# In the mixer: one channel group's filter moved to ScalarE and GpSimd, the channel norm ahead of the attention units, output halves one per unit

## The reference, cut to what matters

```python
h = xn @ w_in
glu_a, glu_g, c_q, c_kv, k_r = jnp.split(h, SPLIT_EVEN, axis=-1)
u = glu_a * jax.nn.sigmoid(glu_g)
u = causal_dwconv(u, conv_w, conv_b)                    # 31 taps, each channel by itself
u = jax.nn.silu(layer_norm(u, conv_ln_g, conv_ln_b))
q = (rms_norm_2(c_q, q_norm) @ w_uq).reshape(b, s, N_HEADS, 96)
q_nope, q_rope = q[..., :QK_NOPE_DIM], rope(q[..., QK_NOPE_DIM:], pos)
kv = (rms_norm_2(c_kv, kv_norm) @ w_ukv).reshape(b, s, N_HEADS, 128)
k_nope, v = kv[..., :QK_NOPE_DIM], kv[..., QK_NOPE_DIM:]
k_rope = rope(k_r[:, :, None, :], pos)[:, :, 0, :]
attn = mla_attention(q_nope, q_rope, k_nope, k_rope, v)  # causal, 4 blocks of 128 rows
return jnp.concatenate([u, attn], axis=-1) @ w_out
```

## Time and profile before

| | us |
|---|---|
| median of 3 runs | 2725.79 (2721.75 to 2727.71) |
| the profiled execution, its own time | 2724.76 |
| its span, first to last instruction | 2722.3 |
| PE busy in the span | 2653.7 (97%) |
| DVE, ACT, POOL busy | 1329.2, 623.9, 317.1 |
| the mixer's part in question, from 1523.4 to 1731.6 | 208.2 |

### The profile page before, as it was taken

One profiled execution on the slowest core, in us unless ns is written; L12 is line 12 of the kernel. 1 busy time (PEld: TensorE's weight loads), 2 busy tenths in 40 slices (PEclk: granted clock), 3 DMA queues, 4 the chain that ended last, 5 costly groups with the idle time before them and its releaser, 6 DMA issues.

```text
span 2722.3 us, 31881 instructions
## 1 busy us (share of the span) xinstructions
PE 2653.7 (97%) x12378; PEld 1844.2 (68%) x12378; DVE 1329.2 (49%) x2850; ACT 623.9 (23%) x1152; POOL 317.1 (12%) x313
## 2 busy tenths in 40 slices
PE   8999999999999999999999998999999999999998
PEld 4777658898895655444444445588884484888887
DVE  2255556566552013000013776477666673877733
ACT  1155532313321112110001134222220022222201
POOL 0222124434342410000000000000000000000000
PEclk9999989999999998999999998999999999999999
DMA  4211111111012220344433210122223211222222
GB/s 190 78 47 63 47 47 47 43 36 47 32 47 93 94 95 32 124 170 170 170 116 108 78 62 16 70 78 93 93 81 120 96 63 62 78 93 93 78 93 93
DMA packets 32494, 226.98 MB, mean 83 GB/s; under 512 B 3552, under 2 KB 4192, under 8 KB 6112
## 3 DMA queue, kind: packets, MB, share of 16 engines
q1 hardware_dynamic: 30384, 219.50, 22.5%
q10 hardware_dynamic: 1968, 5.51, 0.6%
HBM read 222.90 MB, written 2.10 MB: 83 GB/s over the span
## 4 chain that ended last, share of the span: by engine, by line
PE 92%; DVE 4%; ACT 2%; issue 1%; POOL 0%; DMA 0%; ACTq 0%; DVEq 0%; POOLq 0%
PE psum L400 90%; DVE work L2721 1%; PE psum L899 1%; PE psum L1226 0%; DVE work L1802 0%; PE psum L2248 0%; PE psum L2577 0%; DVE work L1050 0%; DVE hT L572 0%; DVE work L1796 0%; ACT work L613 0%; DMA mixT<-x_dram 0%; PE psum L636 0%; PE psum L1892 0%; ACT work L965 0%
## 5 line engine op out<-in xcount | busy, mean ns | idle before, releaser
L400 PE MATMUL psum<-hT,ring 128*128 128x256 f32 (+2 forms) x2872 | 542.8, 370 | 10.8 <-ACT work L1351 6.1
L400 PEld LDWEIGHTS psum<-hT,ring 128*128 128x128 f32 (+1 forms) x2872 | 375.9, 162 | 143.7 <-issue 95.4
L400 PE MATMUL psum<-work,ring 128*128 128x512 f32 (+1 forms) x1208 | 418.5, 498 | 4.8 <-ACT work L3506 2.4
L400 PEld LDWEIGHTS psum<-work,ring 128*128 128x128 f32 x1208 | 228.3, 190 | 178.7 <-issue 156.4
L400 PE MATMUL psum<-work 128*128 128x128 f32 (+7 forms) x2390 | 326.8, 290 | 10.3 <-ACT work L2682 6.6
L400 PEld LDWEIGHTS psum<-work 128*128 128x128 f32 (+2 forms) x2390 | 275.2, 178 | 62.3 <-issue 31.9
L400 PE MATMUL psum<-work,mixT 128*128 128x256 f32 (+2 forms) x1332 | 289.2, 379 | 2.7 <-ACT work L2101 1.5
L400 PE MATMUL psum<-xT,ring 128*128 128x256 f32 (+1 forms) x1120 | 285.1, 400 | 1.4 <-ACT mixT L754 1.3
L400 PEld LDWEIGHTS psum<-work,mixT 128*128 128x128 f32 (+1 forms) x1332 | 232.1, 182 | 49.2 <-issue 16.1
L400 PE MATMUL psum<-ring,work 128*128 (+1 forms) x568 | 248.7, 596 | 2.2 <-issue 1.9
L400 PEld LDWEIGHTS psum<-xT,ring 128*128 128x128 f32 x1120 | 206.1, 190 | 53.2 <-issue 26.4
(11 more groups left out here) (450 smaller groups left out, 2740.9 us busy)
## 6 DMA issues: line engine op xcount, KB each, us to landing
ring<-stream_dram SPq DMA_DIRECT2D x204, 1024.0 KB, 4.8
con<-consts_dram SPq DMA_DIRECT2D x1, 2953.0 KB, 13.4
mixT<-x_dram ACTq DMA_DIRECT2D x4, 512.0 KB, 6.2
work<-x_dram ACTq DMA_DIRECT2D x4, 512.0 KB, 5.9
out_dram<-mixT SPq DMA_DIRECT2D x4, 512.0 KB, 3.7
work<-p_dram ACTq DMA_DIRECT2D x1, 512.0 KB, 3.9
con<-ssm_dram ACTq DMA_DIRECT2D x1, 512.0 KB, 4.2
vec<-vecs_dram SPq DMA_DIRECT2D x1, 378.0 KB, 5.7
```

Of the source, the lines that this page charges most:

```text
L400: ins = self.eng.matmul(out, lhsT, rhs, start=start, stop=stop)
```

## The change

It touches the mixer alone. Group 1's 31 taps (`POOL_TAPPED = 1`) leave DVE. ACT makes the scaled, shifted copy of each tap (`tap_products`), into one of four buffers, and POOL adds it to `ys` (`taps_pool`), 30 additions in a chain. ACT's 31 products stand behind its gate tiles 1, 2 and 3 and its two query latents, and from tap 5 on each waits until POOL has done tap t-4. The gate and up tiles of group 3 now come right behind those of group 2, and the weight stream has its slots in that order. PE does the diagonal products, the mean, and the sum of squares between the projections instead of in the loop, and the first four output products ahead of unit 0; in the loop it does one output product per unit, to unit 27. DVE subtracts the mean and scales between the rotary additions, and does no tap in the loop. POOL spreads the rotary key over the heads (a copy of 32x4096) in ACT's place.

```diff
-    for j in range(3):
+    for j in range(4):
...
-    gated(3)
...
+        POOL_TAPPED, TAPPED_ORDER = 1, (0, 2, 3)
+        HALF_FIRST, HALF_LAST, TURN_AT = 4, 27, (12, 20, 28)
+        filter_bank = psum[:, 2, :]
...
-            for j in range(1, 3):
-                w = slot()
...
+            for j in range(1, 4):
                 w = slot()
                 tile_pe(blocks(w, 0, 8), h)
                 tile_pe(blocks(w, 8, 8), h)
             w = slot()
             tile_pe(blocks(w, 0, 8), h)
-            for k in range(3):
+            tile_pe(blocks(w, 8, 8), h)
+            e.eng.wait_ge(S["keys_act"], KEYS_STEP["diagonals"])
+            e.eng.wait_ge(S["tile_free"], e.c["tile"].at(-2))
+            for t in range(PE_TAPS):
+                ins = e.mm(filter_bank, diag[:, t, :], upad[:, 3, t:t + T], t == 0, t == PE_TAPS - 1)
+            ins.then_inc(S["ln_pe"], 1)
+            for k in range(2):
                 e.eng.wait_ge(S["squares"], TILES + k + 1)
-                ins = col_sums_pe(e, squares[:, 4 + k, :], mean_col(256 if k < 2 else 128), 0 if k < 2 else NB, k == 0, k == 2)
+                ins = col_sums_pe(e, squares[:, 4 + k, :], mean_col(256), 0, k == 0, k == 1)
             ins.then_inc(S["col_sums"], 1)
+            w = slot()
             e.eng.wait_ge(S["tile_free"], e.c["tile"].at(-1))
             o = e.bank()
...
-                if k == 4:
+                if k == 5:
                     e.eng.wait_ge(S["col_root"], e.c["col_root"].next())
...
-                    root_rows_pe(e, root_bank, 0)
-                    root_rows_pe(e, root_bank2, NB).then_inc(S["mla_root"], 1)
-                ins = e.mm(o, blk(w, 8 + k), h[k], k == 0, k == DC - 1)
+                    root_rows_pe(e, root_bank, 0).then_inc(S["mla_root"], 1)
+                ins = e.mm(o, blk(w, k), h[k], k == 0, k == DC - 1)
             ins.then_inc(S["tile_done"], 1)
+            tile_pe(blocks(w, 8, 8), h)
+            e.eng.wait_ge(S["squares"], TILES + 3)
+            col_sums_pe(e, squares[:, 6, :], mean_col(128), NB, True, True).then_inc(S["col_sums"], 1)
+            for n, j in enumerate((*TAPPED_ORDER[:2], POOL_TAPPED, TAPPED_ORDER[2])):
+                if j == POOL_TAPPED:
+                    e.eng.wait_ge(S["mix_pool"], MIX_POOL["channel"])
+                else:
+                    e.eng.wait_ge(S["channel"], TAPPED_ORDER.index(j) + 1)
+                ins = e.mm(aux_banks[0], mean_of(512), ys[:, j, :], n == 0, n == 3)
+            ins.then_inc(S["ln_pe"], 1)
...
             for n in range(8):
                 tile_pe(blocks(w, 2 * n, 2), [cq[:, k, :] for k in range(2)])
+                if n == 3:
+                    e.eng.wait_ge(S["col_root"], e.c["col_root"].next())
+                    root_rows_pe(e, root_bank2, NB).then_inc(S["mla_root"], 1)
+                if n == 4:
+                    for k in range(4):
+                        e.eng.wait_ge(S["ln_act"], LN_ACT["squares"] + k + 1)
+                        ins = e.mm(aux_banks[0], mean_of(512), squares[:, k, :], k == 0, k == 3)
+                    ins.then_inc(S["ln_pe"], 1)
...
-            e.eng.wait_ge(S["keys_act"], KEYS_STEP["k_spread"])
+            e.eng.wait_ge(S["mix_pool"], MIX_POOL["k_spread"])
             scores(0)
             scores(1)
-            for k in range(3):
-                e.eng.wait_ge(S["channel"], k + 1)
-                e.mm(aux_banks[0], mean_of(512), ys[:, k, :], k == 0, False)
+            e.eng.wait_ge(S["ln_act"], LN_ACT["out"])
+            aux.half_out(e, HALF_FIRST)
...
-                if u < PE_TAPS:
-                    if u == 0:
...
-                    if u == OUT_AT:
-                        e.eng.wait_ge(S["ln_act"], 1 + 4 + 1 + 4)
-                    if u in (22, 26):
-                        aux.turned(e, 1 if u == 22 else 2)
-                    aux.half_out(e, 2)
...
+                if u <= HALF_LAST:
+                    aux.half_out(e, 1)
...
-            for j in range(1, 3):
+            def tap_products(e, first, end):
+                e.eng.wait_ge(S["tile_free"], upad_at)
+                for t in range(first, end):
+                    w = taps_w[:, POOL_TAPPED, t:t + 1]
+                    if t >= 5:
+                        e.eng.wait_ge(S["mix_pool"], MIX_POOL["taps"] + t - 4)
+                    if t == 0:
+                        ins = nc.scalar.activation(ys[:, POOL_TAPPED, :], upad[:, POOL_TAPPED, 0:T], ACT.Identity, scale=w,
+                                                   bias=V("conv0_b")[:, POOL_TAPPED:POOL_TAPPED + 1])
+                    else:
...
+                    ins.then_inc(S["ln_act"], 1)
...
+            for j in range(1, 4):
                 gate(j)
+                if j == POOL_TAPPED:
+                    upad_at = e.c["tile"].at()
+                if j >= POOL_TAPPED:
+                    tap_products(e, *((0, 5), (5, 15), (15, 24))[j - POOL_TAPPED])
             for k, dst in enumerate((cq[:, 0, :], cq[:, 1, :], ckv)):
                 whole(dst)
                 e.eng.wait_ge(S["tile_free"], e.c["tile"].at())
                 nc.scalar.activation(squares[:, 4 + k, :], dst, ACT.Square).then_inc(S["squares"], 1)
+                if k < 2:
+                    tap_products(e, *((24, 29), (29, 31))[k])
+                if k == 1:
+                    col_sqrt_act(e, 0, NB, C("eps")[:, 0:1])
             e.skip(1)
...
+            for k in range(4):
+                e.eng.wait_ge(S["ln_dve"], k + 1)
+                nc.scalar.activation(squares[:, k, :], ys[:, k, :], ACT.Square).then_inc(S["ln_act"], 1)
...
+            for k in range(4):
+                e.eng.wait_ge(S["ln_dve"], LN_DVE["scaled"] + k + 1)
+                nc.scalar.activation(catT[:, k, :], ys[:, k, :], ACT.Silu, bias=V("ln_b")[:, k:k + 1])\
+                    .then_inc(S["ln_act"], 1)
             mla_act(e)
...
+        def taps_pool(e):
+
+            y = ys[:, POOL_TAPPED, :]
+            for t in range(1, 31):
+                e.eng.wait_ge(S["ln_act"], t + 1)
+                if t > 1:
+                    e.eng.wait_ge(S["mix_pool"], MIX_POOL["taps"] + t - 1)
+                nc.gpsimd.tensor_tensor(y, y, squares[:, t % 4, :], ALU.add).then_inc(S["mix_pool"], 1)
+            e.eng.wait_ge(S["rope"], KEY_ROPE)
+            e.eng.wait_ge(S["mix_pool"], MIX_POOL["channel"])
+            nc.gpsimd.tensor_copy(kh[64:96, :, :], bc1(kr[64:96, :], MH)).then_inc(S["mix_pool"], 1)
...
-            e.eng.wait_ge(S["gate_rooted"], 2)
+            e.eng.wait_ge(S["mix_pool"], MIX_POOL["gate_up"])
             gated(0)
+            taps.some(e, 16)
+            gated(1)
+            taps.some(e, 15)
+            gated(2)
             taps.some(e, 17)
-            gated(1)
-            taps.some(e, 17)
-            gated(2)
-            taps.some(e, 34)
+            gated(3)
+            taps.some(e, 14 + 13)
+            col_root_dve(e, 0, NB)
+            taps.some(e, 3)
+            e.eng.wait_ge(S["mla_root"], e.c["mla_root"].next())
+            for k in range(2):
+                nc.vector.scalar_tensor_tensor(out=cq[:, k, :], in0=cq[:, k, :], scalar=V("mla_q")[:, k:k + 1], in1=root_bank,
+                                               op0=ALU.mult, op1=ALU.mult).then_inc(S["latents"], 1)
+            taps.some(e, 7 + 1)
...
-            taps.some(e, 4)
-            e.eng.wait_ge(S["mla_root"], e.c["mla_root"].next())
...
+            e.eng.wait_ge(S["ln_pe"], LN_PE["mean"])
+            for j in range(4):
+                if j == POOL_TAPPED:
+                    e.eng.wait_ge(S["mix_pool"], MIX_POOL["channel"])
+                nc.vector.tensor_tensor(ys[:, j, :], ys[:, j, :], aux_banks[0], ALU.subtract).then_inc(S["ln_dve"], 1)
...
+                if n == 0:
+                    e.eng.wait_ge(S["mla_root"], e.c["mla_root"].next())
+                    nc.vector.scalar_tensor_tensor(out=ckv, in0=ckv, scalar=V("mla_kv"), in1=root_bank2, op0=ALU.mult,
+                                                   op1=ALU.mult).then_inc(S["latents"], 1)
+            e.eng.wait_ge(S["ln_act"], LN_ACT["root"])
+            for j in range(4):
+                nc.vector.scalar_tensor_tensor(out=ys[:, j, :], in0=ys[:, j, :], scalar=V("ln_g")[:, j:j + 1],
+                                               in1=rstd, op0=ALU.mult, op1=ALU.mult).then_inc(S["ln_dve"], 1)
```

More of the change, by code:

```diff
@@ L2452, in program @@
         SO_FAR, TURNED = UNITS_A, UNITS_A + 2 * NB
-        TAPS_AT, MEAN_AT, SUMS_AT, ROOT_AT, OUT_AT = 9, 9, 11, 13, 16
+        LN_PE, LN_ACT, LN_DVE = {"filter": 1, "mean": 2, "sums": 3}, {"squares": 31, "root": 36, "out": 40}, {"scaled": 4}
+        MIX_POOL = {"gate": 1, "gate_up": 2, "taps": 2, "channel": 32, "k_spread": 33}
+        POOL_TAPPED, TAPPED_ORDER = 1, (0, 2, 3)
+        HALF_FIRST, HALF_LAST, TURN_AT = 4, 27, (12, 20, 28)
+        filter_bank = psum[:, 2, :]
         aux_banks = (psum[:, 1, :], psum[:, 3, :])
@@ L2508, in mixer_pe @@
             e.eng.wait_ge(S["h_ready"], e.c["h_ready"].at())
```

(18 more changed lines are left out.)

100 lines of the change are left out of this document (30 added, 70 removed).

## The result

| | before | changed |
|---|---|---|
| median | 2727.82 us, 16 runs (2721.75 to 2730.83) | 2731.89 us, 16 runs (2729.48 to 2734.80) |
| ratio | | 1.0016, 95% interval 1.0009 to 1.0024 |
| span of the profiled execution | 2722.3 | 2731.5 |

The changed kernel is 4 us slower, 0.16%: clear of the noise of 16 runs, and inside the 0.2% that was named as the bound of what counts.

The account below looks back on a forecast made before the run. PE was taken as the bound: its work, waits and low-clock stretches. The profiled execution's 2724.76 plus 2.2 (idle PE against a shorter loop) plus 3.4 (clock) gave 2730.4; with the median 1.0 above, 2731.5 us, range 2713 to 2741.

Parts of the forecast that it names:

- The price of 1.68 us per pair: Mixer's filter: one DVE tap and one POOL addition take 1.68 us together while both have work; bounds 1.61 and 2.02.
- third gated product ends, after the first one's start: DVE's list: slowed taps make the third gated product end at 39.1 us, while PE has gate 3 done at 34.2.
- root of the query latents: DVE's list: after 27 more taps, ending at 88.3 us, comes the root; PE reaches its place at 80.7.
- idle PE at the three places: Ahead of the loop, PE idles 4.9, 7.9 and 7.8 us: before up 3, the second query latent, and within `ckv`.
- first transposes: Start of the attention loop: 1641.7 if nothing else holds PE up, 1662.3 with 20.6 us of idle PE ahead.
- loop to residual: Attention loop, first transposes to residual products: 71.5 us against 101.9, with one output product in each of 28 units.
- the mixer's end against before: Residual at 1733.8 against 1731.64, so +2.2 us, plus +3.4 for slow clock.
- The slow clock behind the small products: Ahead of scores, a half tile took 5.38 us instead of 3.45; 1.9 us taken as gone, large products now standing there.
- The step on the rotary key: Spreading the key on POOL: 7.6 or 10.2 us at most, hidden before scores; counted 0, with 3 kept for the range.
- No contention that matters: Filter: POOL adds between undisturbed taps at 1.35 us, PE never idles for them; 2709 us. Chance 0.15 including its half way.
- POOL loses to DVE: Filter: taps stay quick, POOL's additions fall behind, PE waits for ACT and the mean instead; 2725 to 2735 us. Chance 0.05.
- The worse cases: Pair of 1.9 to 2.02 us or longer low clock: 2738 to 2740, both 2745; 0.15 shared with an unshortened loop.

## Why the prediction was right

It forecast 2731.5 us, and 2731.89 was measured. As a difference it forecast 5.7 us (2731.5 less 2725.79), and the medians of 16 runs differ by 4.1. Of its three outcomes it gave "slower", by more than 0.2%, the best chance (0.47) and "same" 0.34; the measured 0.16% is "same", 1.4 us short of the bound. The mechanism is what it said. The price of 1.68 us per pair was read from rows of another stage; the measured period is 1.67 to 1.70. By its steps:

| step | forecast | measured |
|---|---|---|
| third gated product ends, after the first one's start | 39.1 | 38.6 |
| fourth | 60.8 | 60.7 |
| root of the query latents | 88.3 | 88.0 |
| idle PE at the three places | 4.9, 7.9, 7.8 | 4.5, 5.2, 5.3 |
| first transposes | 1662.3, with the clock 1665.7 | 1665.9 (2.5 taken off) |
| loop to residual | 71.5 | 70.6 |
| the mixer's end against before | +5.6 | +4.8, +6.0 behind the residual |

DVE's list came out within 0.5 us everywhere. The idle times sum up to 15.0 us instead of 20.6. They are shorter than forecast at the second and third place, and the difference is the clock: behind each wait PE ran at 0.50 for 3.5 us, so it came to the next wait later and waited less there. The prediction said that a slow clock behind the first two waits costs little; the sum bears it out. What it priced wrongly is small. It gave the loop 0.9 us too much. The slow clock behind the small products was gone, as it assumed: ten records behind them took 4.54 us, where eight had taken 5.38. It missed the slow clock in the residual, behind the waits of the last units (28.88 us instead of 27.63, where 64 records stand).

The 36.1 us ahead of the loop come apart as the windows above have it: 13.9 more of idle PE and 22.3 more of busy PE. Of the busy part 14.7 is work moved there (17 products of 0.86), and of the rest, 7.6, most is a low clock: three stretches of 3.5 us and one of about 3 us at half speed cost 6.8, the 23 us at 0.92 to 0.93 behind them 1.8, less the 1.9 of before. The 31.3 us won in the loop are read from the windows alone; no run takes the taps, the mean and the second output product out of the loop one by one.

The step on the rotary key was right to count nothing: POOL took 3.59 us for it, as ACT had before, and nobody waited.

```profile
1629.40 3.59 POOL L2716 COPY work<-work 32x4096 f32<-32x4096 f32 x1 [28.13 <-DVE work L2807]
```

The rivals. "No contention that matters" was forecast at 2709 and did not happen, but it is what the kernel with the sum in PSUM does, at 2710.46, so its price was right as well. It assumed an addition every 1.35 us where nothing disturbs it, and in that run it is 1.41. "POOL loses to DVE" fell: the two alternate. Nor do they exclude each other for the whole of what the trace counts as their duration: that would be 2.02 a pair, and it is 1.68. The worse cases, a pair of 2 us or a long slow stretch, did not come: the loop's clock is 0.99. That the median fits within 0.4 us is luck: the kernel before moved up by 2.0 us between its first three runs and the sixteen, and the difference came out 1.6 us smaller than forecast, and the two cancel. The mixer's own +4.8 in the traces, against +5.6, does not rest on that.

## What to carry to other kernels

Before work is moved from DVE to POOL, look at how many tensors DVE's neighbouring instructions read in SBUF: beside two-read instructions each addition on POOL cost DVE more (0.86 us) than the tap that it saved (0.785). If a PSUM bank is free, a running sum kept there takes DVE out of the collision at nearly no price (756 ns a tap instead of 752, and 0.26 us more for the first operation of a group). Here that made the changed kernel 21 us faster, and the offload, which had been worth nothing, worth 17.6 us. A bound by the order of a list and a bound by its sum have to be worked out apart: curing the order moved three waits into one.

## What the runs showed of the hardware

- DVE with two tensors read in SBUF, and POOL with two: alternately, 1.68 us a pair, where undisturbed a tap comes every 0.785 us and an addition every 1.41. The pair is more than the longer and less than the sum of the bare durations, 0.75 + 1.27 = 2.02. Within a pair the tap lasts 1.64 us and the addition 1.53. With one of DVE's tensors in PSUM there was no slowdown on either side, whether DVE wrote to PSUM (756 ns, additions 1272) or to SBUF (748 and 1275). A gated product, which reads one tensor in SBUF and one in PSUM, took 0.69 us beside the additions as elsewhere.
- A tap with its running sum in PSUM takes 756 ns, with both in SBUF 752. The plain multiply that starts a group takes 0.81 us when it writes to PSUM, and 0.55 to SBUF.
- After 2.5 us of idle PE before the output products, eight records took 5.1 to 6.4 us, and 3.60 without the idle time. Taking 2.4 us of copies from ACT gave 6.4 us back.
